# Where eleven pieces of another product stand among the steps of a triangular inverse

## The reference

```
lower = where(strict, (kbeta @ k^T) * decay, 0)
sol   = triangular_solve(lower + eye, [v * beta, kbeta * exp(g)])
```

## Time and profile before

| what | value |
| --- | --- |
| median of three runs | 1766.57 us |
| the profiled execution | 1765.99 us |
| its span, from the first to the last instruction | 1764.1 us |
| TensorE, matmuls | 1751.2 us, 99% |
| VectorE | 1199.3 us, 68% |
| ScalarE | 959.8 us, 54% |
| GpSimd | 69.8 us, 4% |
| transfers, all queues | 301.24 MB, mean 171 GB/s |

### The profile page before, as it was taken

One profiled execution on the slowest core, in us unless ns is written; L12 is line 12 of the kernel. 1 busy time (PEld: TensorE's weight loads), 2 busy tenths in 40 slices (PEclk: granted clock), 3 DMA queues, 4 the chain that ended last, 5 costly groups with the idle time before them and its releaser, 6 DMA issues.

```text
span 1764.1 us, 35889 instructions
## 1 busy us (share of the span) xinstructions
PE 1751.2 (99%) x15412; PEld 1660.0 (94%) x15412; DVE 1199.3 (68%) x1861; ACT 959.8 (54%) x1508; POOL 69.8 (4%) x32
## 2 busy tenths in 40 slices
PE   9999999999999999999999999999999999999999
PEld 8999998899999999999988899999989989889999
DVE  7775666765766666866577566766674668865676
ACT  6544567455644454545566466444564565655662
POOL 0000011400000000000113100000000000000000
PEclk9999999999999999999999999999999999999999
DMA  9665543333565665555533344556645635556332
GB/s 359 192 193 197 175 153 120 109 118 123 179 193 193 206 207 195 192 193 178 169 130 109 98 155 149 196 192 192 193 166 168 227 108 168 180 167 250 122 120 96
DMA packets 84461, 301.24 MB, mean 171 GB/s; under 512 B 9168, under 2 KB 11728, under 8 KB 84176
## 3 DMA queue, kind: packets, MB, share of 16 engines
q1 hardware_dynamic: 84160, 298.70, 50.9%
q10 hardware_dynamic: 144, 0.26, 0.1%
HBM read 297.88 MB, written 1.05 MB: 169 GB/s over the span
## 4 chain that ended last, share of the span: by engine, by line
PE 94%; DVE 3%; ACT 1%; issue 1%; DMA 0%; DVEq 0%; ACTq 0%
PE bank L408 22%; PE bank L413 21%; PE bank L415 21%; PE bank L433 3%; PE bank L429 3%; PE bank L432 3%; PE bank L748 2%; DVE w_lo L1677 1%; PE bank L675 1%; PE bank L1086 1%; PE bank L679 1%; PE bank L678 1%; PE bank L1137 1%; PE bank L908 1%; PE bank L925 1%; PE bank L1107 1%
## 5 line engine op out<-in xcount | busy, mean ns | idle before, releaser
L1677 DVE TENSOR_TENSOR w_lo<-ring,w_hi 128x1024 fp32r<-128x1024 f32 x541 | 651.0, 1240 | 94.9 <-ACT w_hi L1208 89.8
L1208 ACT ACTIVATE w_hi<-ring 128x1024 fp32r<-128x1024 f32 x541 | 561.8, 1057 | 237.9 <-PE bank L408 185.1
L408 PE MATMUL bank<-xs,w_hi 128*128 128x256 f32 x2160 | 601.5, 278 | 0.7 <-DVE w_lo L1677 0.7
L413 PE MATMUL bank<-xs,w_hi 128*128 128x256 f32 x2165 | 597.4, 276 | 0.0
L415 PE MATMUL bank<-xs,w_lo 128*128 128x256 f32 x2160 | 597.3, 277 | 0.0
L408 PEld LDWEIGHTS bank<-xs,w_hi 128*128 128x128 f32 x2160 | 405.8, 188 | 2.4 <-issue 2.0
L413 PEld LDWEIGHTS bank<-xs,w_hi 128*128 128x128 f32 x2165 | 406.2, 188 | 0.2
L415 PEld LDWEIGHTS bank<-xs,w_lo 128*128 128x128 f32 x2160 | 405.6, 188 | 0.0
L415 PE MATMUL bank<-a,w_lo 128*128 128x256 f32 x704 | 194.3, 276 | 0.0
L408 PE MATMUL bank<-a,w_hi 128*128 128x256 f32 x704 | 194.3, 276 | 0.0
L413 PE MATMUL bank<-a,w_hi 128*128 128x256 f32 x704 | 194.3, 276 | 0.0
(11 more groups left out here) (416 smaller groups left out, 2956.9 us busy)
## 6 DMA issues: line engine op xcount, KB each, us to landing
ring<-in_w SPq DMA_DIRECT2D x557, 512.0 KB, 3.4
arena<-in_mem SPq DMA_DIRECT2D x2, 1024.0 KB, 8.5
const<-in_const SPq DMA_DIRECT2D x1, 1199.0 KB, 6.8
out<-h SPq DMA_DIRECT2D x3, 256.0 KB, 2.5
dec_par<-in_dec SPq DMA_DIRECT2D x1, 695.0 KB, 11.1
h<-in_x SPq DMA_DIRECT2D x1, 512.0 KB, 7.9
h<-in_x SPq DMA_DIRECT2D x1, 260.0 KB, 4.1
ring<-in_w ACTq DMA_DIRECT2D x1, 256.0 KB, 4.3
```

Of the source, the lines that this page charges most:

```text
L408: last = nc.tensor.matmul(o, wh, hi(x, k0 + k), start=k == 0, stop=False, skip_group_check=True)
L413: nc.tensor.matmul(o[:, c:c + piece], wh, lo(x, k0 + k)[:, c:c + piece], start=False, stop=False, skip_group_check=True)
L1208: nc.scalar.activation(w_hi[:, s * UNIT:(s + 1) * UNIT], ring[:, u % RU, :], AF.Copy).then_inc(sems("w_hi"), 1)
L1677: nc.vector.tensor_tensor(w_lo[:, r * UNIT:(r + 1) * UNIT], ring[:, r, :], w_hi[:, s * UNIT:(s + 1) * UNIT].bitcast(F32), ALU.subtract).th ...
```

## The change

Two parts that stood behind both chunks' Y now stand behind one chunk's Y each, in all six levels. Of the three that stood behind both chunks' X Y in levels 1 to 5, one now stands between the chunks and two behind them. In level 6 the one part behind X Y stays. The number of parts and their order among themselves are the same, and no other engine's list is touched.

```diff
                             four(2 + c, c, ct[:, lv % 2, :], xx, "y_full", n)
                         else:
                             corner(2 + c, c, ct[:, lv % 2, :], xx, "y_full", 0, P // 2)
-                    values_part(2)
+                        values_part(1)
                     for c in range(2):
                         pe.e.wait_ge(*pe.need('yy', 2 * lv + c - 1))
                         if lv < LEVELS - 1:
                             four(6 + c, c, yy, xt, "xyt_full", n)
                             four(4 + c, c, xt, yy, "xy_full", n)
+                            values_part(1 + c)
                         else:
                             corner(6 + c, c, yy, xt, "xyt_full", P // 2, 0)
-                    values_part(3 if lv < LEVELS - 1 else 1)
+                    if lv == LEVELS - 1:
+                        values_part(1)
```

## The result

The changed kernel took 1774.18 us as the median of five runs (1771.14 to 1774.50). Its ratio to the kernel before is 1.0040, with a 95% interval of 1.0029 to 1.0052: slower by 7.6 us, where 6.7 were forecast. In a second series of seven runs the median was 1774.39 and the ratio 1.0041 (1.0025 to 1.0057).

A forecast was written before the change was run, and what follows sets the result against it. TensorE was taken as the bound, busy 1751.2 of 1764.1 us. Terms 5.2 + 0.9 + 2.8 - 3.8 + 1.6 = +6.7 on the profiled 1765.99 gave 1772.7, plus 0.58 for the median 1773.3; range 1766.5 to 1779.0.

The forecast's parts named there:

- (a): TensorE, levels 2 to 6: each added pair of switches between parts and narrow tile products costs 0.29 us, +5.2 us.
- (b): Level 1: covered only by Y0, the first part waits 0.45 us for its weights' low halves, +0.9 in two layers.
- (c): Level 5: the first part waits longer for low halves that GpSimd holds up on VectorE, +1.6 and +1.2, together +2.8 us.
- (d): TensorE's four packet stalls in the stage: two go, two shrink; with the clock fall behind one (-1.6), sum -3.8 us.
- (e): Level 5, first layer: the new 1.9 us wait lowers the clock, +1.6 us; second layer 0.
- R3: Rival, whole stage: switches between parts and tile products are free; with (b), (c) and all stalls gone, -0.7, 1765.9; chance 0.12.

The follow-up runs named there:

- experiment 1: Only the first half of the edit (one part behind each chunk's Y) on the kernel before: 1772.42 us, ratio 1.0029.
- experiment 2: Only the second half of the edit (a part between the chunks' X Y) on the kernel before: 1768.23 us, ratio 1.0004.
- experiment 5: The kernel before, old order, with 128x128 tile products in levels 2 to 5 too: 1782.33 us, ratio 1.0090.
- experiment 6: The new order with 128x128 tile products in levels 2 to 5 too: 1786.50 us, ratio 1.0117.
- experiment 3: The changed kernel with GpSimd's split for the output projection moved ahead of level 5's mask: 1771.12 us, ratio 1.0018.
- experiment 4: Only the second half of the edit on the kernel before, with GpSimd's split moved ahead of level 5's mask: 1767.05 us, ratio 1.0002.
- experiment 8: The kernel before with 20 repeats of one sum, 80 TensorE instructions, ahead of the second layer's levels: 1775.64 us in one run.
- experiment 7: The changed kernel again, unedited, in a second series of seven runs with a second profile: 1774.39 us (1770.96 to 1775.70).

## Why the prediction was right, and where it was not

Measured from the first pair of profiles, as differences of level lengths:

| step | forecast, us | measured, us | how |
| --- | --- | --- | --- |
| (a) switches | +5.2 | +5.9 | 6 x 0.60 in levels 2 to 4; 2 x 0.69 in level 5 without its wait; 2 x 0.35 in level 6; 2 x 0.09 in level 1 |
| (b) level 1's low halves | +0.9 | +0.9 | 2 x 0.45 |
| (c) level 5's low halves | +2.8 | +2.6 | waits 1.81 and 1.14, less 0.38 before |
| (d) packet stalls | -2.2 | -2.0 | level excess 4.5 before, 2.5 after |
| (d) clock behind them | -1.6 | -1.6 | 9.03 - 5.81 - 1.64 of stall |
| (e) clock behind level 5's wait | +1.6 | 0 | window below |
| not forecast: decoder, clock | 0 | +3.4 | 771.21 - 767.85 |
| not forecast: ahead of the stage | 0 | -0.6 | starts 324.48 and 323.85 |

**(a) right.** A pair cost 0.30 us with 32-wide tiles, 0.35 with 64-wide ones and next to nothing with 128-wide ones, so R3's free switches are refuted by experiments 1, 2, 5 and 6. The Trainium skill, TensorEngine Tiling (Array Packing), Key Properties, says that a change of mode, not of tile, drains TensorE. The 0.60 us against 0.03 for the same two splits agrees, though no run here keeps the width and changes the mode alone.

**(b) and (c) right**, with the mechanisms shown. The timeline of TensorE in level 1, to be read against the earlier trace rows: the part waits until 325.14, where the burst alone would have let it start at 323.85 + 0.85 = 324.70.

```profile
323.85 1.05 PE L748 MATMUL bank<-arena,sq 128*128 128x128 f32 x8
325.14 0.51 PE L675 MATMUL bank<-w_hi,ms 128*128 128x512 f32 x1 [0.24 <-DVE w_lo L1679]
```

The bracket gives 0.24, the starts give 0.44; the modelled end of the burst hides the rest. In level 5, 355.47 - 353.06 less the burst's 0.60 is 1.81 us, against the 1.9 forecast, with 1.14 in the second layer. Level 2's rest of a stall stands in the same view:

```profile
338.29 0.45 PE L748 MATMUL bank<-arena 32*32 32x32 f32 x30 [0.37 <-issue]
...
353.06 0.68 PE L748 MATMUL bank<-arena,sq 64*64 64x64 f32 x16
355.47 0.51 PE L675 MATMUL bank<-w_hi,ms 128*128 128x512 f32 x1 [1.73 <-DVE w_lo L1679]
```

That GpSimd's subtraction held VectorE's low half is shown by experiment 3.

**(d) right in its sum, not in its parts.** The level lengths put the stalls at 4.5 us before, where the brackets, which the forecast took, give 3.5: a bracket leaves out part of a stall. For the longest, the burst below to the part at 338.57 is 2.91 us, 1.64 over the 1.27 of an undisturbed one.

```profile
335.66 1.10 PE L748 MATMUL bank<-arena 32*32 32x32 f32 x101
```

The 1.44 us stall shrank to 0.37 (0.7 was forecast), and the 0.51 and the 0.69 went. The last, from which 0.6 was to be left of 0.87, became 0.42 and brought another:

```profile
982.09 0.25 PE L748 MATMUL bank<-arena,sq 32*32 32x32 f32 x3 [1.07 <-issue]
...
985.84 0.28 PE L748 MATMUL bank<-arena 32*32 32x32 f32 x9 [0.42 <-issue]
987.64 0.68 PE L748 MATMUL bank<-arena,sq 64*64 64x64 f32 x16
989.39 0.50 PE L675 MATMUL bank<-w_hi,ms 128*128 128x512 f32 x1 [1.07 <-DVE w_lo L1679]
```

From three records left in Y1 to nine left in XY1 are 3 + 3 + 64 + 3 + 55 = 128 records: the border between the two counted packets. Before, it lay at the end of a Y burst and held TensorE for 0.14 us, too little for the lists. I had counted only the borders with a listed stall, and a nearly silent one can be moved into a place where it stalls. In two of the experiments too a stall appeared where I hadn't put one (1.74 in experiment 2, 1.45 in experiment 4), and in experiment 8 one of 1.35 us stood where 0.8 was expected. Where borders lie can be counted; how long a packet takes to come was not predicted to better than about a microsecond.

The traces also time the packets of the instruction queue (queue 8 of the page), which the forecast didn't use, and they bear its step out: in each of the 27 stalls over 0.1 us of this stage, over eight profiles, TensorE went on 1.27 to 1.61 us after such a packet had landed (for the 1.44 us stall it landed at 336.87, and TensorE went on at 338.21). The packet itself took 0.88 to 1.36 us. What varied most is when it set out: 0.97 to 2.58 us after the border 128 records ahead of the stall. What decides that stays open. The Trainium skill, Runtime: NRT & Kernel Launch, Instruction fetch mechanics, holds that crossing a block is mostly hidden. The stalls that moved by 40 records with 80 instructions show the opposite for a stream of 32x32 products.

**(e) failed in its place.** Behind the 1.73 us wait the first profile has full clock:

```profile
355.40:359.00 3.60, 3.53 (x55) 2.56 (x55) 1.15 (x2) 1.54 (x2) 0.00 (x0) 1.00 0.44 146
```

In the second profile it fell to 0.58. Falls followed stalls or waits of 1.44, 1.40, 1.72 and 1.74, and none followed 1.27, 1.35, 1.45, 1.69 and 1.73, so length alone does not decide. That the total came out 0.9 us from the forecast owes something to luck: a decoder fall of 3.4 us stood in for the 1.6 that was missing. Without any clock terms the forecast's steps sum to 5.2 + 0.9 + 2.8 - 2.2 = 6.7, against the 6.4 to 6.6 between runs at full clock (lowest runs 1770.96 and 1771.14); that comparison is the fair one. In the profiles two misses that cancel stand in it: (a) came out 0.7 higher than forecast, and 0.6 was saved ahead of the stage, which belongs to the run. The 1.6 that the kernel before lost to the clock in its profile can't have stood in its runs at 1.000, so that term is one of a run, not of the kernel.

**Open.** Why the clock falls in one run at a place and not in the next; and whether the decoder's falls (near 1340 to 1370 or 1590 to 1600 us, in seven of the ten profiles, not in that of the kernel before) have become more frequent with the change or only happened to be in both of its profiles. Experiment 8, in the old order, had one too; in the series of experiment 7, six of twelve runs of the kernel before and one of seven of the changed one were at 1.000, but in the series of experiments 1 to 4 only three of 35 of the kernel before.

## What to carry to other kernels

Spreading filler between the pieces of a chain pays only where the chain is waited for; here no product waited for the copies or updates, so all that the edit could win was in stalls that it moved by accident. Count the changes of tile mode that an order makes (0.3 us a pair here), and ask what the merged burst was covering: the first user of a weight unit was moved ahead of the engine that prepares it. Before reading a difference of a few us in a nearly full TensorE, look where the granted clock fell in each profile, and compare level by level.

## What the runs showed of the hardware that was not expected

- Twenty repeats of one sum, 80 instructions in all, moved the instruction stalls by exactly 40 matmul records, some 1,200 records and 145 us later. Every such stall ended 1.27 to 1.61 us after a packet of the instruction queue had landed. With 128x128 tiles, whose levels last 8.82 us instead of 5.81, no stall was left.
- VectorE's low half, 1.23 us by itself, ended 1.1 us after GpSimd's subtraction ended, whether it started at 354.0 (2.13 us long, before) or at 353.0 (2.42, after).
- The granted clock fell to 0.50 for some 6 us in the decoder with no wait ahead of it.
- One kernel's runs lay between 1763.56 and 1773.07 us with mean granted clocks from 1.000 to 0.995, a spread larger than the effect measured.
